# Reordering the end of the mixer stage: convolution taps, the sum of squares and the order of the four output-projection units

## The chip, the cores and the metric

The kernel runs on one core of a Trainium2 chip. The metric is the device time of one execution in microseconds, the median of three runs. The engines of a core run their own instruction lists side by side and meet only at semaphores: PE (TensorE) multiplies matrices, with the weight load (PEld) as a pipelined part of it, DVE (VectorE) and ACT (ScalarE) do elementwise work and empty the PSUM banks, POOL (GpSimd) and SP (SyncE) mostly start transfers. An engine works through its list strictly in order, so an instruction that waits holds up all behind it.

## The reference

A trunk of two layers on 256 tokens of width 1024. Each layer is a mixer and a channel mixer (dense SwiGLU in layer 0, top-2-of-8 experts in layer 1), then an embedding add. This case is about the mixer, which has three head groups that read one projection of the normed input:

```python
def conformer_conv(u, dw_w, dw_b, ln_g, ln_b):          # 256 columns, group "conv"
    val, gate = jnp.split(u, 2, axis=-1)
    h = causal_depthwise_conv(val * jax.nn.sigmoid(gate), dw_w, dw_b)   # 31 taps
    ...  # mean and variance over groups of 64 channels
    hn = ((hg - mu) * lax.rsqrt(var + LN_EPS)).reshape(b, s, c)
    return jax.nn.silu(hn * ln_g + ln_b)

def ssd_mixer(z, xbc, dt_raw, ...):                      # 512 columns, group "SSD"
    y = ssd_chunked(xs, dt, a, bm, cm) + d_skip[:, None] * xs
    yg = y.reshape(b, s, SSD_WIDTH) * jax.nn.silu(z)
    yg = yg.reshape(b, s, SSD_NGROUPS, SSD_WIDTH // SSD_NGROUPS)
    yg = yg * lax.rsqrt(jnp.mean(yg * yg, axis=-1, keepdims=True) + RMS_EPS)
    return yg.reshape(b, s, SSD_WIDTH) * norm_g
```

The third group is latent attention with 4 heads of 64 value columns (256 columns). The three outputs are concatenated to 1024 columns (0 to 255 conv, 256 to 767 SSD, 768 to 1023 attention) and multiplied by `w_out` (1024 x 1024).

## The kernel before, in words

There is one instruction list per engine, written out by hand in the order in which the engine runs it. Weights come through a ring of 7 slots of 128x2048 words. From the output projection on, each unit of weights is parted in two: ACT copies it to `w_hi` (rounded), DVE subtracts to get `w_lo` (`split`, L1221 on ACT and L1640 on DVE), and a product is three matmuls, hi by hi, hi by lo and lo by hi (L509, L510, L511). The slots of `w_hi` and `w_lo` are three each.

The mixer of a layer runs so. PE makes the input projection unit by unit (conv, small columns, four times xbc, two halves of z), and between them the small products of attention and SSD. DVE spreads the 31 taps of the depthwise convolution (`conv_taps`, L1725, two instructions of 128x256 per tap) over the gaps between its other work: taps 0 to 9, 10 to 16, 17 to 19, 20 to 22, 23 to 25 and 26 to 30. The names that matter at the end of the stage:

- `xdd` (DVE L1863) is the input of the chunk state product `st` (PE L701). The decay matrices are multiplied in place (L1869, "mix"), and `yd` (PE L712) reads them. `yo` (PE L719) comes from the state.
- DVE adds yd, yo and the gate into `ytok` (L1874, L1877, L1879, L1882: `ygz_ready`), subtracts the mean of the convolution (L1887), and normalizes attention's output into `ytok` (L1893).
- ACT squares `ytok` for the SSD norm (L1384, Sqrt in L1388: `grm_ready`), and DVE scales `ytok` (L1897, L1901: `ytok_ready`).
- PE transposes `ytok` in three pairs of 128 columns (`y_transposed`, L743): pair j=2 is attention, 0 and 1 are SSD. ACT takes the hi part (`take_yT`, L1397), DVE the lo part (L1646 or L1647).
- The convolution's branch: ACT squares (L1390), PE sums over groups (L752, "var"), ACT takes the root (L1403), DVE inverts and multiplies (L1919, L1920: `chn_ready`), ACT does Silu and the hi copy (L1410, L1413), DVE the lo part (L1646: `yT_ready`).
- The output projection is four units of 24 matmuls, one for each quarter of the 1024 columns, in `OUT_ORDER`: 3 is attention, 1 and 2 SSD, 0 the convolution. All four add into the same four PSUM banks. Unit i waits for its input parts and for `lo_ready` of its weights, which are the splits `f + 10` to `f + 13`.

After the last unit DVE adds the result to `h` (L1930), and the next norm and its transposes (L527) follow.

Of the kernel before, what the change touches and what calls it, by code (L numbers as in the profile page):

```python
# [82 lines left out]
OUT_ORDER = (3, 1, 2, 0)  # L83
# [34 lines left out]
def trunk(nc, params, x, p, positions, w_in, w_uq, w_ukv, w_out, dense_g, dense_u, dense_d, router,  # L118
          moe_g, moe_u, moe_d, ple_g, ple_p, final_g, out):
    with ExitStack() as ctx:  # L120
# [362 lines left out]
        def _(pe):  # L483
# [91 lines left out]
            def mixers(L):  # L575
# [178 lines left out]
                for j in range(2):  # L754
                    pe.wait_ge(ytok_ready, 2 * L + j + 1)
                    y_transposed(j, 1 + j)
                keys = [("o", L, t, half) for t in range(NT) for half in range(2)]
                acc = {}
                for i, pair in enumerate(OUT_ORDER):
                    w = unit()  # L760
                    if i == 0:
                        pe.wait_ge(*banks.taken(("yT", L, 2)))
                    elif i < 3:
                        pe.wait_ge(*banks.taken(("yT", L, i - 1)))
                    else:
                        pe.wait_ge(yT_ready, L + 1)
                    for n, key in enumerate(keys):
# [443 lines left out]
        def _(act):  # L1211
# [18 lines left out]
            def warmed():  # L1230

                act.wait_ge(table_in, warmings[0])
# [46 lines left out]
            def mixers(L):  # L1279
# [29 lines left out]

                act.wait_ge(dtn_ready, L + 1)  # L1310
                A(dte, dtn, ACT.Exp).then_inc(dte_ready, 1)
                A(nega, lp(L, "alog", 0, SH), ACT.Exp).then_inc(nega_ready, 1)
                act.wait_ge(pads_ready, L + 1)
                take_xbc(0)
# [66 lines left out]
                act.wait_ge(ygz_ready, L + 1)  # L1381
                for t in range(NT):
                    for g in range(SG):
                        A(dx[:, t, g * SEQ:g * SEQ + SEQ], ytok[:, t, g * SEQ:g * SEQ + SEQ], ACT.Square,  # L1384
                          accum_out=gss[:, 2 * t + g:2 * t + g + 1]).then_inc(gss_ready, 1)
                act.wait_ge(gss_ready, 4 * (L + 1))
                warmed()
                A(grm, gss, ACT.Sqrt, scale=SG / SSDW, bias=eps_rms).then_inc(grm_ready, 1)  # L1388
# [12 lines left out]
                take_yT(2)  # L1401
                o = banks.filled(act, ("var", L))
                A(csq.rearrange("p m s -> p (m s)"), o, ACT.Sqrt, bias=eps_ln).then_inc(  # L1403
                    banks.is_free(("var", L)), 1)
                for j in range(2):
                    take_yT(j)
# [6 lines left out]
                A(yT_hi[:, 0:2, :], csq, ACT.Copy).then_inc(conv_hi_ready, 1)  # L1413

# [193 lines left out]
        def _(dve):  # L1608
# [101 lines left out]
            def mixers(L):  # L1710
# [64 lines left out]
                conv_taps(10, 17)  # L1775
                xbc_taps(0)
                conv_taps(17, 20)
# [34 lines left out]
                conv_taps(20, 23)  # L1812
                xbc_taps(3)
                split(f + 10)
                conv_taps(23, 26)
# [37 lines left out]
                for t in range(NT):  # L1853
                    for g in range(SG):
                        o = banks.filled(dve, ("seg", L, t, g))
                        for i in range(4):
                            hd = 4 * g + i
                            c = t * SH + hd
                            last = V.tensor_scalar(dec[:, t, hd, :], o[:, i * P:i * P + P], acs[:, c:c + 1], 0.0,
                                                   ALU.subtract, ALU.min)  # L1860
                        last.then_inc(banks.is_free(("seg", L, t, g)), 1)
                dve.wait_ge(ea_ready, L + 1)
# [8 lines left out]
                conv_taps(26, CK)  # L1871
# [24 lines left out]
                dve.wait_ge(grm_ready, L + 1)  # L1896
                step(V.reciprocal(grs, grm))  # L1897
                for g in range(SG):
                    for t in range(NT):
                        v = ytok[:, t, g * SEQ:g * SEQ + SEQ]  # L1900
                        last = V.tensor_scalar(v, v, grs[:, 2 * t + g:2 * t + g + 1], None, ALU.mult)  # L1901
                    last.then_inc(ytok_ready, 1)
# [12 lines left out]
                for j in range(2):  # L1915
                    take_yT(j, 2 + j)
                split(f + 12)
# [4 lines left out]
                rest(yT_lo[:, 0:2, :], csq, yT_hi[:, 0:2, :]).then_inc(yT_ready, 1)  # L1922
                for i in range(13, 16 if L == 0 else 14):
                    split(f + i)
# [376 lines left out]
```

## Time and profile before

| | |
|---|---|
| median of 3 runs | 1562.73 us (1561.97 to 1563.8) |
| profiled execution: its own time | 1562.73 us |
| profiled execution: span of the trace | 1560.9 us |
| busy: PE / DVE / ACT | 1476.2 / 1188.9 / 1013.4 us |
| mean granted TensorE clock | 0.988 |

The span is what the trace shows from the first to the last instruction. The profiled execution took 1.83 us more than its span. Busy time is the time in which an engine had an instruction in work. A timeline row gives the start and the length of one or several like instructions on one engine and, in brackets, how long the engine was idle before it and who released it. The input and mixer stage lies at 0 to 143 us (layer 0) and about 408 us later in layer 1; the dense channel mixer and the embedding lie between, the experts after 578 us.

### The profile page before, as it was taken

The page shows a single profiled execution, that of the slowest core. Times are in us where ns is not written, and L with a number is a line of the kernel's source. Part 1 is how long each engine was busy: PE and PEld are TensorE (multiplying, and loading weights), DVE is VectorE, ACT ScalarE, POOL GpSimd, SP SyncE. Part 2 cuts the span into 40 slices and gives each one's busy share as a digit, 9 for nine tenths or more (in the row PEclk, how much of TensorE's full clock was granted, in tenths as well). Part 3 has the DMA queues.
Part 4 walks back from the last instruction along what each step waited for, and adds up shares of the span by engine and source line. Part 5 has one row for each costly group of instructions (what it writes and reads, how often), then busy time and mean ns, then how long its engine had stood idle before and what let it go on. Part 6 is the DMA issues. An engine that isn't in the chain of part 4 may idle for free.

```text
span 1560.9 us, 18290 instructions
## 1 busy us (share of the span) xinstructions
PE 1476.2 (95%) x6932; PEld 1194.4 (77%) x6932; DVE 1188.9 (76%) x1113; ACT 1013.4 (65%) x947; POOL 9.3 (1%) x21
## 2 busy tenths in 40 slices
PE   6998999999899969999999999999999999999987
PEld 5767888887777758887778887778887778887766
DVE  2796455544457758889998988998979998978994
ACT  3465444434426537768887768887768887768883
POOL 0000000000000000000000000000000000000000
PEclk9999999999999979999999999999999999999999
DMA  8335555555241059999999999999999999999971
GB/s 294 135 109 185 164 188 188 188 189 179 82 137 53 1 198 403 355 356 389 394 395 397 363 348 378 389 394 401 353 354 375 387 401 395 361 354 380 384 289 40
DMA packets 143670, 441.80 MB, mean 283 GB/s; under 512 B 6928, under 2 KB 21296, under 8 KB 143584
## 3 DMA queue, kind: packets, MB, share of 16 engines
q1 hardware_dynamic: 142832, 438.24, 76.1%
q0 software_dynamic: 752, 2.39, 0.4%
q8 instruction: 56, 0.92, 0.2%
q14 instruction: 30, 0.25, 0.0%
HBM read 439.56 MB, written 1.05 MB: 282 GB/s over the span
## 4 chain that ended last, share of the span: by engine, by line
PE 75%; DVE 13%; ACT 7%; issue 5%; DMA 0%; DVEq 0%; ACTq 0%; SPq 0%
PE psum L509 16%; PE psum L511 16%; PE psum L510 16%; DVE w_lo L1640 9%; PE psum L545 5%; ACT w_hi L1221 5%; PE psum L943 4%; PE psum L944 4%; PE psum L559 3%; PE psum L527 2%; PE psum L987 2%; PE psum L902 1%; PE psum L911 1%; PE psum L981 1%; DVE hidden_a L1646 1%
## 5 line engine op out<-in xcount | busy, mean ns | idle before, releaser
L1640 DVE TENSOR_TENSOR w_lo<-ring,w_hi 128x2048 fp32r<-128x2048 f32 x396 | 900.0, 2289 | 241.2 <-ACT w_hi L1221 240.4
L1221 ACT ACTIVATE w_hi<-ring 128x2048 fp32r<-128x2048 f32 x396 | 755.5, 1915 | 283.9 <-PE psum L511 249.5
L511 PE MATMUL psum<-w_hi,hidden_b 128*128 128x512 f32 x560 | 219.1, 391 | 0.0
L943 PE MATMUL psum<-w_hi,xT_parts 128*128 128x512 f32 x448 | 193.3, 431 | 10.9 <-DVE w_lo L1640 10.8
L509 PE MATMUL psum<-w_hi,hidden_b 128*128 128x512 f32 x448 | 178.7, 399 | 7.3 <-DVE w_lo L1640 7.3
L944 PE MATMUL psum<-w_lo,xT_parts 128*128 128x512 f32 x448 | 175.6, 392 | 0.0
L510 PE MATMUL psum<-w_lo,hidden_b 128*128 128x512 f32 x448 | 175.2, 391 | 0.0
L509 PE MATMUL psum<-w_hi,hidden_a 128*128 128x512 f32 x352 | 138.0, 392 | 3.2 <-DVE hidden_a L1646 3.2
L509 PE MATMUL psum<-w_hi,xT_parts 128*128 128x512 f32 x352 | 137.9, 392 | 2.2 <-DVE w_lo L1640 1.8
L511 PE MATMUL psum<-w_hi,xT_parts 128*128 128x512 f32 x352 | 137.1, 389 | 0.0
L510 PE MATMUL psum<-w_lo,xT_parts 128*128 128x512 f32 x352 | 137.0, 389 | 0.0
L510 PE MATMUL psum<-w_lo,hidden_a 128*128 128x512 f32 x352 | 137.0, 389 | 0.0
L511 PEld LDWEIGHTS psum<-w_hi,hidden_b 128*128 128x128 f32 x560 | 105.6, 188 | 22.4
L943 PEld LDWEIGHTS psum<-w_hi,xT_parts 128*128 128x128 f32 x448 | 84.2, 188 | 42.1 <-DVE w_lo L1640 21.2
L509 PEld LDWEIGHTS psum<-w_hi,hidden_b 128*128 128x128 f32 x448 | 84.7, 189 | 26.5 <-DVE w_lo L1640 8.7
L944 PEld LDWEIGHTS psum<-w_lo,xT_parts 128*128 128x128 f32 x448 | 84.3, 188 | 21.1 <-issue 6.2
L510 PEld LDWEIGHTS psum<-w_lo,hidden_b 128*128 128x128 f32 x448 | 84.7, 189 | 16.6
L962 PE MATMUL psum<-w_hi,hidden_a 128*128 128x512 f32 x224 | 92.7, 414 | 4.0 <-DVE w_lo L1640 2.5
L511 PE MATMUL psum<-w_hi,hidden_a 128*128 128x512 f32 x240 | 93.5, 390 | 0.0
L963 PE MATMUL psum<-w_lo,hidden_a 128*128 128x512 f32 x224 | 87.8, 392 | 0.0
L545 PE MATMUL psum<-xT,ring 128*128 128x256 f32 x384 | 84.2, 379 | 0.0
L545 PEld LDWEIGHTS psum<-xT,ring 128*128 128x128 f32 x384 | 72.7, 190 | 11.1 <-issue 1.6
(305 smaller groups left out, 1636.6 us busy)
## 6 DMA issues: line engine op xcount, KB each, us to landing
ring<-in_moe_w_gate SPq DMA_DIRECT2D x112, 1024.0 KB, 7.3
ring<-in_moe_w_up SPq DMA_DIRECT2D x112, 1024.0 KB, 7.5
ring<-in_moe_w_down SPq DMA_DIRECT2D x112, 1024.0 KB, 7.7
ring<-in_w_in SPq DMA_DIRECT2D x16, 1024.0 KB, 5.4
ring<-in_dense_w_gate SPq DMA_DIRECT2D x14, 1024.0 KB, 5.1
ring<-in_dense_w_up SPq DMA_DIRECT2D x14, 1024.0 KB, 5.2
ring<-in_dense_w_down SPq DMA_DIRECT2D x14, 1024.0 KB, 4.8
ring<-in_w_out SPq DMA_DIRECT2D x8, 1024.0 KB, 4.9
```

The source lines that it names most:

```text
L509: mm(o, a[0], b[0], start=first, stop=False)
L510: mm(o, a[0], b[1], start=False, stop=False)
L511: return mm(o, a[1], b[0], start=False, stop=final)
L527: last = mm(o[:, c:c + P], h[:, t, kt * P:kt * P + P], diag[:, t, :], start=True, stop=True)
L545: last = mm(o[:, m * SEQ:m * SEQ + SEQ], w[:, kt, m * P:m * P + P], xT[:, kt, :], start=kt == 0, stop=kt == KT - 1)
L559: last = mm(o[:, 0:n], xT[:, kt, t * P:t * P + P], w[:, q, :], start=kt == 0, stop=kt == KT - 1)
L943: mm(o, xl_hi_lo[kt], w[0][:, q, c], start=kt == 0, stop=False)
L944: last = mm(o, xl_lo_hi[kt], w[1][:, q, c], start=False, stop=kt == KT - 1)
L962: mm(o, elT_hi_lo[kt], w[0][:, q, c], start=kt == 0, stop=False)
L963: last = mm(o, elT_lo_hi[kt], w[1][:, q, c], start=False, stop=kt == FKT - 1)
L1221: A(part(w_hi, g, sizes[g]), raw(g, sizes[g]), ACT.Copy).then_inc(hi_ready, 1)
L1640: V.tensor_tensor(part(w_lo, g, sizes[g]), raw(g, sizes[g]), f32(part(w_hi, g, sizes[g])), ALU.subtract).then_inc(lo_ready, 1)
```

## The change

The change reorders instructions. The count of rows on each engine stays as it was (975 rows on DVE). It has four parts.

1. ACT takes xbc unit 0 (`take_xbc(0)`, L1304 and L1306) ahead of the two Exp for `dt` and the decay rate (L1311, L1312).
2. The convolution's taps are cut otherwise: 10 to 13, 14 to 17, 18 to 20, 21 to 24, and the last six (25 to 30) stand before `xdd` instead of the last five after the mixes.
3. The order of the output projection is attention, convolution, SSD, SSD. PE transposes the two SSD pairs after the first unit.
4. On ACT the squares of `ytok` come after `take_yT(2)`, and `take_yT(0)` and `take_yT(1)` after the convolution's Silu. On DVE `split(f + 11)` and `take_yT(2)` come ahead of the scaling of `ytok`, and the convolution's branch ahead of `split(f + 12)` and the two SSD pairs.

```diff
-OUT_ORDER = (3, 1, 2, 0)
+OUT_ORDER = (3, 0, 1, 2)
@@ PE
-                for j in range(2):
-                    pe.wait_ge(ytok_ready, 2 * L + j + 1)
-                    y_transposed(j, 1 + j)
...
                     if i == 0:
                         pe.wait_ge(*banks.taken(("yT", L, 2)))
-                    elif i < 3:
-                        pe.wait_ge(*banks.taken(("yT", L, i - 1)))
-                    else:
+                    elif i == 1:
+                        for j in range(2):
+                            pe.wait_ge(ytok_ready, 2 * L + j + 1)
+                            y_transposed(j, 1 + j)
                         pe.wait_ge(yT_ready, L + 1)
+                    if i > 1:
+                        pe.wait_ge(*banks.taken(("yT", L, i - 2)))
@@ ACT
+                act.wait_ge(pads_ready, L + 1)
+                take_xbc(0)
                 act.wait_ge(dtn_ready, L + 1)
                 A(dte, dtn, ACT.Exp).then_inc(dte_ready, 1)
                 A(nega, lp(L, "alog", 0, SH), ACT.Exp).then_inc(nega_ready, 1)
-                act.wait_ge(pads_ready, L + 1)
-                take_xbc(0)
...
                 warm_up()
-                act.wait_ge(ygz_ready, L + 1)
...
-                A(grm, gss, ACT.Sqrt, scale=SG / SSDW, bias=eps_rms).then_inc(grm_ready, 1)
                 act.wait_ge(*banks.taken(("mean", L)))
...
                 take_yT(2)
+                act.wait_ge(ygz_ready, L + 1)
...
+                A(grm, gss, ACT.Sqrt, scale=SG / SSDW, bias=eps_rms).then_inc(grm_ready, 1)
                 o = banks.filled(act, ("var", L))
...
-                for j in range(2):
-                    take_yT(j)
                 split(f + 12)
...
                 A(yT_hi[:, 0:2, :], csq, ACT.Copy).then_inc(conv_hi_ready, 1)
+                for j in range(2):
+                    take_yT(j)
@@ DVE
-                conv_taps(10, 17)
+                conv_taps(10, 14)
                 xbc_taps(0)
-                conv_taps(17, 20)
+                conv_taps(14, 18)
...
-                conv_taps(20, 23)
+                conv_taps(18, 21)
                 xbc_taps(3)
                 split(f + 10)
-                conv_taps(23, 26)
+                conv_taps(21, 25)
...
+                conv_taps(25, CK)
                 dve.wait_ge(ea_ready, L + 1)
...
-                conv_taps(26, CK)
```

The end of DVE's list is moved in the same way (part 4), and the rows below show it.

The first place is DVE between the decay matrices and the mixes of a layer (L1859 or L1861 writes the decay matrices, L1863 or L1866 is `xdd`, L1869 or L1872 the four mixes, L1725 or L1727 the taps). Before:

```order
L1859 TENSOR_SCALAR arena_a<-psum,tiny 128x128 [waits full2]
L1859 TENSOR_SCALAR arena_a<-psum,tiny 128x128 x3
L1863 TENSOR_TENSOR xs<-arena_b,tiny 128x512 [waits ea_ready]
L1869 TENSOR_TENSOR arena_a<-arena_a,arena_b 128x512 [waits dec_ready] x4
L1725 SCALAR_TENSOR_TENSOR arena_a<-arena_a,par 128x256 x2
```

After:

```order
L1861 TENSOR_SCALAR arena_a<-psum,tiny 128x128 [waits full2]
L1861 TENSOR_SCALAR arena_a<-psum,tiny 128x128 x3
L1727 SCALAR_TENSOR_TENSOR arena_a<-arena_a,par 128x256 x2
L1727 SCALAR_TENSOR_TENSOR arena_a<-arena_a,par 128x256 [waits dve_step]
L1727 SCALAR_TENSOR_TENSOR arena_a<-arena_a,par 128x256
```

Before, `xdd` and the mixes follow at once and ten tap instructions stand behind them. Now twelve tap instructions stand ahead of `xdd`, of which the first four are shown, and nothing stands between the mixes and L1874.

The second place is the end of DVE's mixer list, from the normalized attention output (L1893 or L1895) on. Before:

```order
L1893 TENSOR_TENSOR xs<-psum,tiny 128x256
L1897 RECIPROCAL tiny<-tiny 128x4 [waits grm_ready]
L1901 TENSOR_SCALAR xs<-xs,tiny 128x256 [waits dve_step]
L1901 TENSOR_SCALAR xs<-xs,tiny 128x256 x3
L1640 TENSOR_TENSOR w_lo<-ring,w_hi 128x2048 [waits hi_ready]
L1646 TENSOR_TENSOR xT_parts<-psum,xT_parts 128x256 [waits full0,y_hi_ready]
```

After:

```order
L1895 TENSOR_TENSOR xs<-psum,tiny 128x256
L1642 TENSOR_TENSOR w_lo<-ring,w_hi 128x2048 [waits hi_ready]
L1648 TENSOR_TENSOR xT_parts<-psum,xT_parts 128x256 [waits full0,y_hi_ready]
L1648 TENSOR_TENSOR xT_parts<-psum,xT_parts 128x256
L1911 RECIPROCAL tiny<-tiny 128x4 [waits grm_ready]
L1915 TENSOR_SCALAR xs<-xs,tiny 128x256 [waits dve_step]
L1915 TENSOR_SCALAR xs<-xs,tiny 128x256 x3
L1918 RECIPROCAL arena_a<-arena_a 128x512 [waits free5]
L1919 TENSOR_TENSOR arena_a<-arena_a 128x512 [waits dve_step]
L1648 TENSOR_TENSOR xT_parts<-arena_a,xT_parts 128x512 [waits conv_hi_ready]
```

The five instructions of the SSD norm moved behind the split and attention's lo part, and the convolution's reciprocal follows them directly. `split(f + 12)` and the SSD pairs come after all of it.

## Rows read from the trace of the kernel before

**Rows 1.** The page's parts 1 and 4: busy time, and the chain by engine.
```profile
PE 1476.2 (95%) x6932; PEld 1194.4 (77%) x6932; DVE 1188.9 (76%) x1113; ACT 1013.4 (65%) x947; POOL 9.3 (1%) x21
PE 75%; DVE 13%; ACT 7%; issue 5%; DMA 0%; DVEq 0%; ACTq 0%; SPq 0%
```

**Rows 2.** Chain in order of time, 105 to 120 us: start, us, what.
```profile
108.63 0.70 DVE xs L1877
...
111.34 0.04 ACT arena_b L1384
```

**Rows 3.** Timeline, 45 to 80 us, ACT and DVE: start, us, engine, line.
```profile
46.47 1.28 ACT L1311 ACT_TABLE_LOAD   x1
...
48.05 0.16 DVE L1773 TENSOR_SCALAR tiny<-tiny 128x16 f32<-128x16 f32 x1
...
52.84 0.60 ACT L1306 ACTIVATE arena_a<-psum 128x512 f32<-128x512 f32 x1
...
62.23 0.18 DVE L1783 TENSOR_TENSOR tiny<-tiny 128x16 f32<-128x16 f32 x1 [1.52 <-ACT tiny L1323]
...
72.52 2.71 DVE L1725 SCALAR_TENSOR_TENSOR arena_a<-arena_a,par 128x256 f32<-128x256 f32 x6
...
79.16 0.88 DVE L1738 SCALAR_TENSOR_TENSOR arena_a<-arena_a,par 128x256 f32<-128x256 f32 x2 [3.93 <-ACT arena_a L1306]
```

**Rows 4.** Timeline, 80 to 111 us: DVE and the PE weight loads.
```profile
83.99 2.71 DVE L1725 SCALAR_TENSOR_TENSOR arena_a<-arena_a,par 128x256 f32<-128x256 f32 x6
...
86.98 0.18 DVE L1818 COPY tiny<-psum 128x24 f32<-128x24 f32 x1 [0.29 <-PE psum L629]
...
99.27 0.68 DVE L1863 TENSOR_TENSOR xs<-arena_b,tiny 128x512 f32<-128x512 f32 x1
...
102.28 4.54 DVE L1725 SCALAR_TENSOR_TENSOR arena_a<-arena_a,par 128x256 f32<-128x256 f32 x10
...
103.02 0.73 PEld L701 LDWEIGHTS psum<-xs,arena_b 128*128 128x128 f32 x4
...
107.45 0.73 PEld L719 LDWEIGHTS psum<-arena_b,arena_a 128*128 128x128 f32 x4
```

**Rows 5.** Timeline, 110 to 130 us: the start of the output projection.
```profile
112.18 0.76 DVE L1893 TENSOR_TENSOR xs<-psum,tiny 128x256 f32<-128x256 f32 x2 [0.16 <-PE psum L734]
...
114.68 2.29 DVE L1640 TENSOR_TENSOR w_lo<-ring,w_hi 128x2048 fp32r<-128x2048 f32 x1
...
114.91 1.04 PE L743 MATMUL psum<-par,xs 128*128 128x128 f32 x8
...
116.88 0.75 DVE L1646 TENSOR_TENSOR xT_parts<-psum,xT_parts 128x256 fp32r<-128x256 f32 x2
...
117.73 0.47 PE L509 MATMUL psum<-w_hi,xT_parts 128*128 128x512 f32 x1 [1.78 <-DVE w_lo L1640]
...
121.31 3.35 DVE L1919 RECIPROCAL arena_a<-arena_a 128x512 f32<-128x512 f32 x1
...
123.27 0.39 PE L509 MATMUL psum<-w_hi,xT_parts 128*128 128x512 f32 x1
...
127.21 0.69 DVE L1646 TENSOR_TENSOR xT_parts<-arena_a,xT_parts 128x512 fp32r<-128x512 f32 x1 [1.82 <-ACT xT_parts L1413]
```

**Rows 6.** Timeline: first projection matmul of layer 1, norm transposes of both layers.
```profile
143.13 6.62 PE L527 MATMUL psum<-xs,h 128*128 128x128 f32 x32 [3.37 <-DVE xs L1632]
...
525.45 0.47 PE L509 MATMUL psum<-w_hi,xT_parts 128*128 128x512 f32 x1 [0.42 <-issue]
...
550.26 3.84 PE L527 MATMUL psum<-xs,h 128*128 128x128 f32 x32 [0.86 <-DVE xs L1632]
```

**Rows 7.** Windows of 1 us: busy time of each engine, granted clock (PEclk), DMA.
```profile
112.00:113.00 1.00, 0.08 (x2) 0.01 (x1) 0.77 (x3) 1.00 (x6) 0.00 (x0) 1.00 0.00 0
148.00:149.00 1.00, 1.00 (x6) 1.00 (x6) 0.69 (x2) 0.35 (x1) 0.00 (x0) 0.50 0.88 244
521.00:522.00 1.00, 0.87 (x5) 0.47 (x4) 0.84 (x4) 1.00 (x4) 0.00 (x0) 0.53 0.00 0
```

More of the change, by code:

```diff
@@ L1380, in mixers @@
                 warm_up()
-                act.wait_ge(ygz_ready, L + 1)
[L1382 to L1387, printed above, removed]
-                A(grm, gss, ACT.Sqrt, scale=SG / SSDW, bias=eps_rms).then_inc(grm_ready, 1)
                 act.wait_ge(*banks.taken(("mean", L)))
@@ L1401, in mixers @@
                 take_yT(2)
+                act.wait_ge(ygz_ready, L + 1)
+                for t in range(NT):
+                    for g in range(SG):
+                        A(dx[:, t, g * SEQ:g * SEQ + SEQ], ytok[:, t, g * SEQ:g * SEQ + SEQ], ACT.Square,
+                          accum_out=gss[:, 2 * t + g:2 * t + g + 1]).then_inc(gss_ready, 1)
+                act.wait_ge(gss_ready, 4 * (L + 1))
+                warmed()
+                A(grm, gss, ACT.Sqrt, scale=SG / SSDW, bias=eps_rms).then_inc(grm_ready, 1)
                 o = banks.filled(act, ("var", L))
@@ L1895, in mixers @@
                 last.then_inc(banks.is_free(("pv", L)), 1)
[L1896 to L1902, printed above, removed]
                 split(f + 11)
@@ L1914, in mixers @@
                 take_yT(2, 1)
-                for j in range(2):
-                    take_yT(j, 2 + j)
-                split(f + 12)
+                dve.wait_ge(grm_ready, L + 1)
+                step(V.reciprocal(grs, grm))
+                for g in range(SG):
+                    for t in range(NT):
+                        v = ytok[:, t, g * SEQ:g * SEQ + SEQ]
+                        last = V.tensor_scalar(v, v, grs[:, 2 * t + g:2 * t + g + 1], None, ALU.mult)
+                    last.then_inc(ytok_ready, 1)
                 dve.wait_ge(*banks.taken(("var", L)))
@@ L1922, in mixers @@
                 rest(yT_lo[:, 0:2, :], csq, yT_hi[:, 0:2, :]).then_inc(yT_ready, 1)
+                split(f + 12)
+                for j in range(2):
+                    take_yT(j, 2 + j)
                 for i in range(13, 16 if L == 0 else 14):
```

## The prediction

> **What bounds the kernel now.** I read the page's busy times first, then the chain, then the timeline around the changed places. PE is busy 95% of the span and is 75% of the chain [rows 1]: the kernel is a row of products, and what a change at another engine is worth shows only where PE has to stand still or is made to run a product later. The chain in order of time shows where that is in the mixer: it runs on PE through the small products and leaves it after yo, whose load is at 107.45 us [rows 4], for DVE's L1877 at 108.6 us [rows 2]. It is back on PE at 117.73 us, where the first projection unit starts after an idle of 1.78 us [rows 5]. From there the four units run without a gap (the 25th matmul, the first of the second unit, starts at 123.27 us, 5.54 us after the first). Before 108 us PE has no wait for DVE at the state product: its weight load stands at 103.02 us, while xdd was written at 99.95 us [rows 4]. So DVE is ahead there by 3.1 us, and behind from 108.6 us on. Layer 1 repeats this 407.72 us later: its first projection matmul is at 525.45 us [rows 6]. Each cost below is taken twice.
>
> All that follows is in the profiled execution's own time, 1562.73 us, of which 1560.9 us are its span and 1.83 us lie outside; that is also the median of the runs.
>
> **Part 1: xbc ahead of the Exp.** DVE's L1773 at 48.05 us waits for the Exp, and all later taps stand behind it. ACT now first waits for the xbc bank, whose evacuation ends at 52.84 + 0.60 = 53.44 us, then loads the table, 1.28 us, and does the Exp (0.22 us, an estimate from the gap of rows 3 between the table load's end at 47.75 us and 48.05 us with the handover). DVE goes on at about 55.0 us, 7.0 late. What covers it: until 79.16 us DVE has two taps fewer, four instructions of 2.71 / 6 = 0.452 us, 1.8 us; and it was idle 1.52 us at 62.23 us. The taps that ended at 75.23 us end at 75.23 + 7.0 - 1.8 - 1.5 = 78.9 us at the latest, and DVE waited for ACT until 79.16 us anyway, 3.93 us [rows 3]. I take 0. If the cover fell short, it would be by tenths, and each tenth would be added to the next part. From below: nothing starts sooner by it, since PE does not wait for xbc here.
>
> **Part 2: the taps.** Four taps instead of three stand before L1818. They would end at 83.99 + 8 x 0.452 = 87.6 us, and L1818 was at 86.98 us: +0.6 us. From there to xdd DVE has no idle worth naming, so xdd is due at 99.9 us. But now twelve tap instructions are ahead of it: 12 x 0.454 = 5.45 us (4.54 us for ten, rows 4). xdd starts at 105.35 and ends at 106.03 us. PE asks for it at 103.02 us, now idles 3.0 us, and all behind it on PE (yd, yo, mean, attention's product) moves by 106.1 - 103.0 = +3.1 us. The mixes, 2.5 us in all, are done at 108.5 us, each one before yd needs it: yd starts 0.8 us after st and takes 3.7 us. The ten tap instructions that stood behind the mixes lay beside yd and cost nothing there (102.28 to 106.8 us, and yo was not before 107.45 us). So the move takes work out of a covered place and puts it in front of PE. The bounds are 0 (had PE been later by 3.1 us) and 5.45 + 0.6 = 6.05 us; I take 3.1 us, since both ends of the wait have a row.
>
> **Part 4 on DVE, up to the first unit.** L1893 ended at 112.94 us and moves with yo to 116.0 us. Behind it the split starts at once; with 116.88 - 114.68 = 2.20 us for it and 0.75 us for attention's lo part the bank is free at 119.0 us and unit 0 starts at 119.1 us [rows 5]. That is +1.35 us against 117.73 us: taking the SSD norm out of the way gives back 1.7 us of the 3.1.
>
> **Part 3, the second unit.** The eight transposes of SSD, 1.04 us [rows 5], ran while PE waited for DVE anyway. Now they stand between unit 0 and unit 1: 119.1 + 5.5 = 124.6 us, then 125.65 us. Unit 1 is now the convolution's and waits for the last step of its branch. That branch is long: from the reciprocal (3.35 us, starts 121.31 us) to the lo part's end (127.90 us) it takes 6.59 us [rows 5]. It can start now when DVE has scaled ytok. PE's four transposes of attention (about 0.6 us, half of the 1.04 and a handover) and ACT's hi part (0.6 us, as L1306 in rows 3) end at about 117.5 us; the four squares, their Sqrt and DVE's scaling take 3.3 us (before, from ACT's first square at 111.34 us [rows 2] to the split behind the scaling at 114.68 us), so about 120.9 us. yT_ready is at 120.9 + 6.6 = 127.5 us, and PE idles about 1.9 us from 125.65 us. Unit 1 starts at 127.55 us instead of 123.27 us: +4.3 us. Had the branch been free, the transposes alone would make it 125.65 us, +2.4 us; with the branch starting later by one split (2.29 us) it would be +6.6 us. I take +4.3 us.
>
> **Units 2 and 3.** DVE does the next split, 2.29 us, and the two SSD pairs, 0.83 us each by the row of attention's 0.75 us, by 131.4 us; PE reaches unit 2 at 133.0 us. They are hidden with 1.6 us to spare. What follows the projection (split, the adds, the norm) is released by PE's units as before. The ring's loads behind `split(f + 12)` on SP's queue start some 8 us later; their weights are used after the norm. So the shift goes on at its full size, into layer 1 and through the experts, where nothing waits for a clock time.
>
> 2 x 4.3 = 8.6 us: 1571.3 us, by the moved instructions alone.
>
> **The clock.** TensorE was granted the lower level (1.2 GHz, 0.50) twice near such idles: at 521 us in layer 1, after a second in which PE did little, and around 142 to 149 us after 3.37 us of idle [rows 6, 7]; yet at 112 us in layer 0, the same place as 521 us, it stayed at 2.4 GHz with PE almost idle for a microsecond. The new idle of 3.0 us at 103 us is nearer to the one of 3.37 us. What it costs: the same 32 transposes took 6.62 us at the lower level and 3.84 us at the full one, so each microsecond at the lower level loses 1 - 3.84 / 6.62 = 0.42 us. The lower level lasted about 5.9 us after work began again at 143.13 us. In the 8.7 us of small products after 106.1 us, all of it ahead of DVE's yo, that is at most 2.5 us and at least 0; I take 5 us, 2.1 us per layer. A fall in the idle of 1.9 us would cost about as much, less likely.
>
> TensorE: Matmul & The Clock Gate of the Trainium skill says in "Part 1: The HAM clock gate" that the throttled state is the default and that activity releases it, so an added idle on PE costs more than its length. The traces agree for two idles and disagree for one. By the rule the sum is 2 x 6.4, without it 2 x 4.3 us.
>
> The sum: 1562.73 + 2 x (4.3 + 2.1) = 1575.5 us.
>
> **Rivals.**
>
> A. The clock stays up at 103 us: 1571.3 us. For it: 112 us, with no fall. Against it: the idle is three times as long.
>
> B. The clock falls at both new idles, in both layers. The second fall costs 2.1 us as well, in units that nothing covers: 1562.73 + 2 x 8.5 = 1579.7 us. For it: in layer 1 a shorter idle was enough. Against it: 24 dense matmuls stand before the 1.9 us.
>
> C. The wait for xdd does not appear, because PE gets to the state product 3.1 us later than I think or DVE has slack that the timeline hides; it decides at 103.02 us. Then unit 0 starts at 116.0 us, 1.7 us earlier than before, its transposes are over at 122.6 us, and the convolution's branch is done at 124.4 us: unit 1 is at 124.5 us, +1.2 us. 1562.73 + 2.4 = 1565.1 us, no change by what can be measured. To be faster the branch must in addition end before the transposes, and then 0.7 us per layer is gained: 1561.3 us. Against it: both sides of the wait have rows, and DVE was without a gap.
>
> D. Part 1 does not stay covered, or an SSD pair is late for unit 2 (DVE has 1.6 us to spare there). If both fail by a microsecond: 1575.5 + 4 = 1579.5 us.
>
> **Chances.** The forecast with a fall at the first idle in one or both layers 0.5; A 0.25; B and D together 0.17; C 0.08. The measurement of this kernel can tell a change of about 0.2%, 3.1 us. C alone lies within it or below; so faster 0.02, same 0.06, slower 0.92. The range of 8 in 10 goes from a little below A, 1569 us, to B, 1580 us.
>
> **What would show it.** DVE should be idle from 48.2 to about 55 us. PE should wait at L701 for about 3 us, released by DVE's xdd. The first projection matmul should start about 1.4 us later than before if the clock held, 3.5 us if not; behind the first 24 there should be eight transposes and an idle of about 2 us released by DVE's lo part of the convolution (little or none of it would say that the branch is quicker than I worked out). The granted clock between 106 and 112 us decides between A and the forecast. I am wrong if xdd stands before 103 us, if unit 1 starts before 125 us, or if the experts' part changes in length.

## The result and the profile after

The changed kernel took 1583.01 us in the median (1580.05 to 1583.84, four runs) and the kernel before 1563.26 us (1561.97 to 1565.76, four runs): a ratio of 1.012, 95% interval 1.0102 to 1.014. A second comparison gave 1581.58 against 1562.79 us, 1.0122 (1.0105 to 1.0139). It is slower, by 19 us; the forecast was 12.8 us and the range ended at 1580 us. The profiled execution was the fastest of the five, 1577.62 us. The page's parts 1 and 4 of the changed kernel:

```profile
span 1575.8 us, 18288 instructions
PE 1483.0 (94%) x6932; PEld 1197.6 (76%) x6932; DVE 1188.2 (75%) x1113; ACT 1013.4 (64%) x947; POOL 9.3 (1%) x21
PE 75%; DVE 13%; ACT 7%; issue 5%; DMA 0%; DVEq 0%; ACTq 0%; SPq 0%
```

The counts are those of before, DVE's and ACT's busy times too [rows 1], but PE was busy 6.8 us longer with the same products: some of them ran slower. The rest of the 14.9 us of span, 8.1 us, is more idle time of PE. The timeline of layer 0, DVE's rows (start, length, and in brackets the idle time ahead and its releaser; L1727 are taps, L1866 `xdd`, L1642 the split, L1648 the lo parts):

```profile
55.23 0.18 DVE L1775 TENSOR_SCALAR tiny<-tiny 128x16 f32<-128x16 f32 x1 [6.87 <-ACT tiny L1314]
...
79.39 0.88 DVE L1740 SCALAR_TENSOR_TENSOR arena_a<-arena_a,par 128x256 f32<-128x256 f32 x2 [1.61 <-ACT arena_a L1306]
...
100.04 5.46 DVE L1727 SCALAR_TENSOR_TENSOR arena_a<-arena_a,par 128x256 f32<-128x256 f32 x12
105.41 0.68 DVE L1866 TENSOR_TENSOR xs<-arena_b,tiny 128x512 f32<-128x512 f32 x1
...
116.00 2.28 DVE L1642 TENSOR_TENSOR w_lo<-ring,w_hi 128x2048 fp32r<-128x2048 f32 x1
118.20 0.75 DVE L1648 TENSOR_TENSOR xT_parts<-psum,xT_parts 128x256 fp32r<-128x256 f32 x2
...
120.70 3.35 DVE L1918 RECIPROCAL arena_a<-arena_a 128x512 f32<-128x512 f32 x1
...
126.59 0.69 DVE L1648 TENSOR_TENSOR xT_parts<-arena_a,xT_parts 128x512 fp32r<-128x512 f32 x1 [1.82 <-ACT xT_parts L1413]
```

The idle of 6.87 us in front of L1775 is the new wait for the Exp. It is gone by L1740 at 79.39 us, where DVE still waits 1.61 us for ACT, as it did before [rows 3]. (This trace is 0.2 us late from its start; each trace has a shift of its own, from 1.5 us earlier to 0.7 us later at L594 in layer 0, which has to be taken off before places are compared.) PE's rows of the same layer:

```profile
106.20 1.10 PE L701 MATMUL psum<-xs,arena_b 128*128 128x256 f32 x4 [2.48 <-issue]
107.14 3.68 PE L712 MATMUL psum<-arena_b,arena_a 128*128 128x64 f32 x32
...
116.14 0.66 PE L743 MATMUL psum<-par,xs 128*128 128x128 f32 x4 [0.92 <-DVE xs L1895]
...
119.04 0.47 PE L509 MATMUL psum<-w_hi,xT_parts 128*128 128x512 f32 x1 [1.39 <-DVE w_lo L1642]
...
124.61 1.04 PE L743 MATMUL psum<-par,xs 128*128 128x128 f32 x8
127.34 0.50 PE L509 MATMUL psum<-w_hi,xT_parts 128*128 128x512 f32 x1 [1.69 <-DVE xT_parts L1648]
```

Layer 0 went as the steps said, to some tenths: the wait at the state product, unit 0 at 119.04 us, the transposes behind it, unit 1 at 127.34 us [rows 4, 5]. The idle is 2.48 us and not 3.0, since PE's products before it run until 103.72 us here. That the 2.48 us at L701 are put down to "issue" must not mislead: no releaser is shown, but DVE's `xdd` ends at 106.09 us and L701 starts at 106.20. The granted clock was 1.00 all the while. Layer 1, the same places:

```profile
516.53 1.10 PE L701 MATMUL psum<-xs,arena_b 128*128 128x256 f32 x4 [2.47 <-issue]
517.47 6.71 PE L712 MATMUL psum<-arena_b,arena_a 128*128 128x64 f32 x32
523.97 2.02 PE L719 MATMUL psum<-arena_b,arena_a 128*128 128x256 f32 x4
...
527.49 3.01 PE L734 MATMUL psum<-arena_b 128*128 128x64 f32 x24
531.41 1.11 PE L743 MATMUL psum<-par,xs 128*128 128x128 f32 x4 [0.92 <-DVE xs L1895]
532.32 1.92 PE L752 MATMUL psum<-arena_a,par 128*128 128x512 f32 x2
```

L712's 32 matmuls took 6.71 us instead of 3.68. The windows (the column after POOL is the granted clock):

```profile
517.00:518.00 1.00, 1.00 (x8) 0.92 (x7) 1.00 (x3) 0.33 (x1) 0.00 (x0) 0.85 0.00 0
518.00:519.00 1.00, 1.00 (x6) 1.00 (x7) 0.83 (x2) 0.98 (x2) 0.00 (x0) 0.50 0.00 0
...
527.00:528.00 1.00, 1.00 (x5) 0.51 (x3) 0.97 (x2) 0.00 (x0) 0.00 (x0) 0.53 0.00 0
528.00:529.00 1.00, 1.00 (x12) 1.00 (x11) 1.00 (x2) 0.00 (x0) 0.00 (x0) 1.00 0.00 0
```

About a microsecond after PE had begun again the clock fell to 0.50 (1.2 GHz), and it stayed there for 10.2 us, from 517.7 to 527.9, though PE had work all the time. From L701 to L743 it is 531.41 - 516.53 = 14.88 us, and in layer 0 116.14 - 106.20 = 9.94: the fall cost 4.94 us.

How the loss adds up along the trace (start of the first matmul of the line named; in the filled version L594 is L601, L527 is L534, L862 is L870 and L902 is L910):

| place | before | after | after, second profile (below) | after with the wait filled (below) |
|---|---|---|---|---|
| layer 0, ahead of the moved instructions' effect (L594) | 59.20 | 59.43 | 58.10 | 58.76 |
| layer 0, behind the projection: the norm's transposes (L527) | 143.13 | 147.33 | 151.41 | 146.65 |
| layer 1, the same (L594) | 466.91 | 469.77 | 475.06 | 470.81 |
| layer 1, behind the projection: gain products (L862) | 547.33 | 559.56 | 564.38 | 555.18 |
| experts' gather (L902) | 567.65 | 580.24 | 585.28 | 576.40 |
| last norm's transposes (L527) | 1525.96 | 1540.85 | 1544.23 | 1534.97 |

From the first row to the second, layer 0's mixer became 3.97 us longer in the first profile (no fall there), 9.38 us in the second and 3.96 us in the filled version; from the third to the fourth, layer 1's became 9.37, 8.90 and 3.95 us longer. So the moved instructions cost 3.96 us in a layer, 7.9 us in all, and a fall the rest. Up to the gain products 12.2 of the 14.9 us have come together. Behind them 2.7 us more came in the first profile: 1.2 us at the experts' start, and 1.5 us at the products of L911, where the granted clock was 0.51 from 1528 to 1530 us and had been 1.00 at the same place of the kernel before. Such a fall at L911 stands in the profile of part 1 alone too (below), and not in the second profile here. Between the experts' start and L911 the expert products took as long as before.

### The profile page after: what moved, and what is told of

Same layout as the page of the kernel before. It is cut to its first block, busy times and chain, and to the rows that moved or that the text cites. A ratio compares the mean times of both kernels' runs of the same rounds, so it can differ in the third digit from the quotient of the medians.

```text
span 1575.8 us, 18288 instructions
## 1 busy us (share of the span) xinstructions
PE 1483.0 (94%) x6932; PEld 1197.6 (76%) x6932; DVE 1188.2 (75%) x1113; ACT 1013.4 (64%) x947; POOL 9.3 (1%) x21
## 4 chain that ended last, share of the span: by engine, by line
PE 75%; DVE 13%; ACT 7%; issue 5%; DMA 0%; DVEq 0%; ACTq 0%; SPq 0%
PE psum L509 16%; PE psum L511 15%; PE psum L510 15%; DVE w_lo L1642 9%; PE psum L545 5%; ACT w_hi L1221 5%; PE psum L943 4%; PE psum L944 4%; PE psum L559 3%; PE psum L987 2%; PE psum L527 2%; PE psum L911 2%; PE psum L902 1%; PE psum L981 1%; DVE hidden_a L1648 1%
## 5 line engine op out<-in xcount | busy, mean ns | idle before, releaser
L1642 DVE TENSOR_TENSOR w_lo<-ring,w_hi 128x2048 fp32r<-128x2048 f32 x396 | 899.7, 2287 | 240.8 <-ACT w_hi L1221 240.0
L943 PEld LDWEIGHTS psum<-w_hi,xT_parts 128*128 128x128 f32 x448 | 84.2, 188 | 42.1 <-DVE w_lo L1642 21.2
L509 PEld LDWEIGHTS psum<-w_hi,xT_parts 128*128 128x128 f32 x352 | 66.2, 188 | 21.8 <-DVE xT_parts L1648 4.1
```

What stands on the lines that cost most here:

```text
L509: mm(o, a[0], b[0], start=first, stop=False)
L943: mm(o, xl_hi_lo[kt], w[0][:, q, c], start=kt == 0, stop=False)
L1642: V.tensor_tensor(part(w_lo, g, sizes[g]), raw(g, sizes[g]), f32(part(w_hi, g, sizes[g])), ALU.subtract).then_inc(lo_ready, 1)
```

## The experiments

All are timed beside the kernel before on the same chip; ratios, not times, are to be compared from one experiment to another. The theory: the moved instructions cost what was worked out, and the clock's fall at PE's new wait costs more than was taken for it. The rivals: the moved instructions cost more (in DVE's later work, or for unit 1), or the four parts hinder one another.

### One part at a time

`taps_only` is the kernel before with part 2 alone:

```diff
-                conv_taps(10, 17) ... conv_taps(17, 20) ... conv_taps(20, 23) ... conv_taps(23, 26)
+                conv_taps(10, 14) ... conv_taps(14, 18) ... conv_taps(18, 21) ... conv_taps(21, 25)
+                conv_taps(25, CK)      # ahead of xdd
-                conv_taps(26, CK)      # behind the mixes
```

> Kernel before with the new cut of the convolution taps alone (10-13, 14-17, 18-20, 21-24, and 25-30 ahead of xdd). Theory T (the wait for xdd costs 3.1 us per layer and then makes the granted clock fall, some 5 us more per layer): 1563 + 2 x 8 = about 1579 us, and in the trace half clock in the small products behind L701 in at least one layer. Rival R1 (the instructions' wait is all that this part costs, the rest of the loss comes from the end of the stage): about 1569 us. Rival R2 (xbc ahead of the Exp is to blame): about 1569 us too.

1573.53 us, ratio 1.0084 (1.0054 to 1.0114). Here it was layer 0 in which the clock fell, PE's rows:

```profile
105.69 1.35 PE L701 MATMUL psum<-xs,arena_b 128*128 128x256 f32 x4 [2.48 <-issue]
106.84 6.93 PE L712 MATMUL psum<-arena_b,arena_a 128*128 128x64 f32 x32
...
120.58 0.65 PE L743 MATMUL psum<-par,xs 128*128 128x128 f32 x4 [0.92 <-DVE xs L1893]
```

14.89 us from L701 to L743 again. In layer 1 of this trace, after the same idle of 2.48 us, L712 took 3.68 us and nothing fell. So the same wait drops the clock in one layer and not in the other, and which one changes. That is one fall where the sum of the expectation had one in each layer (about 1579 us); two of the four executions took 1571.7 us, the others 1575.3 and 1580.1 us.

`tail_only` is the kernel before with parts 3 and 4 (OUT_ORDER and the order of the end of ACT's and DVE's lists):

> Kernel before with the new order of the output projection and of the stage's end on ACT and DVE (parts 3 and 4) alone. Theory T: the branch of the convolution ends late for unit 1, +1.2 us per layer, about 1566 us, first projection matmul at about 116.0 us and unit 1 at about 124.5 us. Rival R1 (the clock falls in the wait between unit 0 and unit 1 and in the emptier end): about 1573 us with half clock in units 1 to 3.

1564.52 us, 1.0016 (1.0006 to 1.0026). Unit 0 was at 115.88 us and unit 1 here:

```profile
124.17 0.50 PE L509 MATMUL psum<-w_hi,xT_parts 128*128 128x512 f32 x1 [1.69 <-DVE xT_parts L1647]
```

That is close to rival C of the prediction in every term (116.0, 124.5 us, +2.4 us), so the convolution's branch and the transposes are priced rightly, to 0.3 us.

`xbc_first_only` is part 1 alone, `take_xbc(0)` ahead of the two Exp:

> Kernel before with ACT taking xbc unit 0 ahead of the two Exp (part 1) alone. Theory T and R1: DVE idles about 7 us at 48 us; with the old cut of the taps the cover is 3.93 + 1.52 + 0.66 + 0.48 = 6.6 us against 7.0, so at most 0.5 us per layer: 1563 to 1565 us. Rival R2: about 1568 us or more.

1562.64 us, 0.9998 (0.9987 to 1.0008): nothing.

The three together are 11.6 + 2.6 us and nothing, 14 us of the 19. The rest is no hindrance of the parts by one another: counted in the traces as in the table above, the mixer is 2.96 and 2.90 us longer with part 2 alone and no fall (`taps_filled`, below) and 1.07 and 1.02 us with parts 3 and 4 alone, together 4.0 us per layer, and all parts at once cost 3.96 us. What differs is the number of falls: one in the two layers of the profile of `taps_only`, three in the four layers of the changed kernel's two profiles. Why there are more with all parts is not shown.

### The wait kept, PE kept busy in it

The changed kernel, with products that nobody reads in PE's wait for `xdd`:

```diff
+            def keep_busy(b, n):
+
+                if banks.count[b]:
+                    pe.wait_ge(banks.free[b], banks.count[b])
+                for _ in range(n):
+                    mm(psum[:, b, :], ones, par[:, 0:512], start=True, stop=True)
...
+                keep_busy(4, n)
                 pe.wait_ge(xdd_ready, L + 1)
```

With n = 6:

> The changed kernel, with six extra matmuls of 128x512 (0.44 us each) on PE into the free bank of st while PE waits for xdd; their results are overwritten. Theory T: the clock stays at the full level in both layers behind L701, and what is left is the instructions' own cost: about 1571 us. Rival R1 (the clock is lost elsewhere, or the fall at xdd is not what costs): it stays at about 1583 us; if the extra matmuls hold PE up, it is more.

1576.3 us, 1.0081 (1.0057 to 1.0105). The clock stayed at 1.00 in both layers, but each call is two instructions of 0.44 us, and the filler was 5.32 us long: it held PE up by itself, and unit 0 was at 121.52 us. The 1571 us that were expected did not come. With n = 3:

> The changed kernel with three products into the state's free bank put in front of PE's wait for xdd, about 2.7 us of work at the higher clock, so that the wait of 2.5 us is filled and not lengthened (six held the first projection unit up to 121.5 us). If the part of the loss above the 8.6 us of moved instructions is the clock's fall after that wait, the granted clock stays 1.00 in both layers from 103 to 115 us, the first projection matmul stands at 119.0 to 119.4 us in layer 0 and at 527 to 528 us in layer 1 (534.3 us in the changed kernel), and the time is 1571 to 1574 us. If the moved instructions alone cost more than worked out (the rival), the clock stays up and the time is still above 1577 us. If small products do not hold the clock, it falls in one layer as before and the time is 1578 to 1583 us.

1569.51 us (1568.7 to 1571.78), 1.0037 (1.0023 to 1.0051). PE's rows of layer 1 (L512 is the filler, L709 the state product, L720 `yd`, L751 the transposes):

```profile
514.94 2.74 PE L512 MATMUL psum<-par 128*128 128x512 f32 x6
517.54 1.13 PE L709 MATMUL psum<-xs,arena_b 128*128 128x256 f32 x4
518.50 3.68 PE L720 MATMUL psum<-arena_b,arena_a 128*128 128x64 f32 x32
...
527.50 0.66 PE L751 MATMUL psum<-par,xs 128*128 128x128 f32 x4 [0.92 <-DVE xs L1903]
```

The state product starts just as late, since `xdd` is no earlier, but it is 9.96 us from L709 to L751, and the time is 12 to 13.5 us less than the changed kernel's, a little under the 1571 to 1574 us expected. Layer 1's first projection matmul, expected at 527 to 528 us, stood at 530.41 us. Part of that is the first profile of the changed kernel, with which it was compared: there the clock had not fallen at layer 0's norm (its 32 transposes took 3.84 us, and 5.47 us here), and the stretch from the second to the third row of the table took 1.7 us less than here. With n = 1:

> The changed kernel with one product (0.9 us) in the wait for xdd instead of three: 1.6 us of idle remain in one piece. If the length of the idle decides whether the clock falls, it falls less often than with 2.5 us: 1571 to 1577 us. If any idle there drops the clock as often, 1580 to 1584 us as in the changed kernel.

1574.68 us (1569.52 to 1580.54), 1.0062 (1.0044 to 1.008). 1.57 us of idle remained. The profiled execution, 1580.54 us, had the fall in both layers; layer 0:

```profile
106.65 1.13 PE L709 MATMUL psum<-xs,arena_b 128*128 128x256 f32 x4 [1.57 <-DVE xs L1874]
107.61 6.17 PE L720 MATMUL psum<-arena_b,arena_a 128*128 128x64 f32 x32
...
121.56 0.66 PE L751 MATMUL psum<-par,xs 128*128 128x128 f32 x4 [0.92 <-DVE xs L1903]
```

14.91 us in each layer (523.23 to 538.14 in layer 1). The fastest execution, at 1569.52 us with a mean clock of 0.992 against 0.983, must have had none; that is read from its mean clock, since it has no profile. By the four times a shorter idle made the fall rarer; by the profile it did not make it cheaper.

The taps' move alone, filled in the same way (n = 3):

> The taps' move alone, with three products (2.7 us) in PE's wait for xdd. The wait itself remains in the time, 3.1 us per layer and 0.6 us of it from the fourth tap: 1562.7 + 6.2 = 1568.9 us. If the clock is what made the taps' move alone cost 11.6 us instead of 6.2, this version takes 1567.5 to 1570.5 us and the granted clock is 1.00 from 103 to 112 us in both layers. If the rest of the 11.6 us is DVE's (a later evacuation, a later norm), it takes 1572 us or more with the clock up.

1568.69 us (1567.95 to 1569.03), 1.0033 (1.002 to 1.0045), where 1568.9 was expected. L751 follows L709 after 9.97 us in both layers. So of part 2's 11.6 us the wait is 5 to 6 (5.4 by these medians, 5.9 by the trace) and the clock the rest. In layer 0 the clock fell later, at the idle of 0.92 us before L751 (0.51 from 117 to 120 us), and it cost nothing: the first unit stands 4.73 us behind L751, and in the kernel before it is 4.74 us behind L743, since PE waits there for DVE anyway.

### The wait taken away

The changed kernel with `conv_taps(25, 28)` ahead of `xdd` and `conv_taps(28, CK)` behind the mixes:

> The changed kernel with six of the twelve tap instructions left ahead of xdd and six behind the mixes. xdd ends 2.7 us earlier, at about 103.3 us, and PE's wait at the state product is 0.3 us or less instead of 3. If the cost is all in that wait and what it does to the clock, then the first unit is at 116.1 us, the second at 124.5 us (the convolution's branch sets it), the clock stays up in both layers, and the time is 1564.5 to 1566.5 us, as the changed tail alone gave. If the clock falls without the wait too, because the other idles of this stretch are enough, the time is 1570 us or more.

1568.03 us (1564.59 to 1569.51), 1.0026 (1.0016 to 1.0035): about 2 us more than worked out. PE had no wait left at L701 (it starts at 102.84 us), but the six taps behind the mixes made the next one longer:

```profile
113.11 1.12 PE L743 MATMUL psum<-par,xs 128*128 128x128 f32 x4 [1.25 <-DVE xs L1896]
114.02 1.92 PE L752 MATMUL psum<-arena_a,par 128*128 128x512 f32 x2
...
124.78 0.50 PE L509 MATMUL psum<-w_hi,xT_parts 128*128 128x512 f32 x1 [2.03 <-DVE xT_parts L1648]
```

1.25 us at L743 instead of 0.92, and in both layers the clock fell at about that place (L752 took 1.92 us and not 1.02). The second half of the expectation ("if the clock falls without the wait too") thus came true in part. Unit 1 is 11.67 us behind L743 in both layers, and 11.20 us in `tail_only`: these falls cost 0.5 us each, through the product of L752, which the convolution's branch waits for. The mixer is 2.1 us longer in each layer than before, 1.0 to 1.1 of it as in `tail_only`; the 0.6 us that are left beside the clock's are DVE's, which gets to L1896 later by the taps.

### The changed kernel a second time

> The changed kernel again, unchanged, for a second profile. In the profiled execution so far (1577.6 us, the fastest of five) the clock fell at the wait for xdd in layer 1 alone and made the stretch from the state product to attention's transposes 14.91 us long instead of 9.97. If the slower executions at 1583 us are those with the fall in both layers, a profile that takes 1580 us or more shows 14.9 us in layer 0 too, and one that takes 1575 to 1578 us shows it in one layer. Rival: the 5 us between them are lost elsewhere (the norm, the experts' start), and a profile above 1580 us still has one such stretch of 9.97 us.

Its profile took 1581.01 us, and the fall is in both layers:

```profile
104.87 1.10 PE L701 MATMUL psum<-xs,arena_b 128*128 128x256 f32 x4 [2.48 <-issue]
105.81 6.86 PE L712 MATMUL psum<-arena_b,arena_a 128*128 128x64 f32 x32
...
119.76 1.11 PE L743 MATMUL psum<-par,xs 128*128 128x128 f32 x4 [0.92 <-DVE xs L1895]
120.66 1.92 PE L752 MATMUL psum<-arena_a,par 128*128 128x512 f32 x2
...
521.84 1.60 PE L701 MATMUL psum<-xs,arena_b 128*128 128x256 f32 x4 [2.48 <-issue]
...
536.72 0.66 PE L743 MATMUL psum<-par,xs 128*128 128x128 f32 x4 [0.92 <-DVE xs L1895]
```

14.89 us in layer 0 and 14.88 in layer 1, as expected of an execution above 1580 us. The windows of layer 0 show 0.50 from 106 to 116 us; the first half:

```profile
106.00:111.00 5.00, 5.00 (x26) 5.00 (x25) 1.87 (x3) 2.08 (x3) 0.00 (x0) 0.50 0.45 169
```

### A version that beats both

Two things in the rows of before pointed to one. PE's first unit waited 1.78 us at 117.73 us [rows 5] for attention's lo part (the row names the split, but the lo part, L1646, ended last, at 117.63 us), which DVE did behind a split of 2.29 us that this unit does not use (it uses `f + 10`). And TensorE ran at the lower level in several stretches behind idles. `lo_first` is the kernel before with one line moved:

```diff
                     last.then_inc(ytok_ready, 1)
-                split(f + 11)
...
                 take_yT(2, 1)
+                split(f + 11)
```

> The kernel before with one line moved: DVE takes attention's lo part before it does the split of the second unit's weights. PE's first unit waited at 117.73 us for whichever of the two came last, and by the order of the units it needs only the lo part. Then attention's lo part ends at 115.4 us, PE has done the eight transposes by 115.9 us, and the first unit starts at 116.0 us instead of 117.7: 1.7 us per layer, 1558.5 us. The second unit then needs the split by 121.5 us (done at 117.7 us) and the first SSD pair (done at 118.5 us). Rival: the split is the first unit's own weights; then nothing starts earlier and the time is the same or 0.7 us per layer longer.

In layer 0 unit 0 started 3.52 us behind DVE's attention rows (L1893 at 112.91, unit 0 at 116.43 us) instead of 5.55 us (112.18 and 117.73): 2.0 us earlier, where 1.7 were expected. The time was 1561.78 us, 0.999 (0.998 to 1.0): 1.3 us less than the kernel before beside it. 1558.5 us were expected, and the interval ends at no change. The rows of layer 1 show why. Of this version:

```profile
518.07 0.99 PE L743 MATMUL psum<-par,xs 128*128 128x128 f32 x4 [0.92 <-DVE xs L1893]
...
522.07 0.48 PE L509 MATMUL psum<-w_hi,xT_parts 128*128 128x512 f32 x1
```

Of the kernel before:

```profile
112.99 0.66 PE L743 MATMUL psum<-par,xs 128*128 128x128 f32 x4 [0.92 <-DVE xs L1893]
...
520.71 0.83 PE L743 MATMUL psum<-par,xs 128*128 128x128 f32 x4 [0.92 <-DVE xs L1893]
```

In both the clock had fallen at the idle of 0.92 us (L752's two products took 2.08 us in each). Before, unit 0 is 4.74 us behind L743 in both layers, with the fall (525.45 us [rows 6]) and without (117.73 us): PE waited for DVE there, so the fall was free. With the lo part early this cover is gone, and unit 0 is 2.71 us behind L743 in layer 0 and 4.00 us in layer 1, where the slow products now decide. Only 0.75 us of the 2.0 were left there.

`before_filled` is the kernel before with fillers in PE's longest idles:

> The kernel before with products of no use put in PE's longest idles ahead of transposes and gathers: three before the norm's transposes in layer 0 (idle 3.37 us), four before the next norm's (4.65 us), seven before the experts' gather (6.99 us) and four behind it (4.81 us). If the clock falls because PE is idle there, it stays at 1.00, the 32 transposes take 3.7 us at 143 us instead of 6.6 and at 422 us instead of 5.4, the gather 3.7 instead of 6.0: about 2.8 + 1.6 + 2.3 us, and some 2 us more in the first expert products, 1554 to 1557 us in all. Rival: the weights' split behind the gather is late whatever the clock, and only 4.4 us or less are gained.

1563.24 us, 0.9992 (0.9982 to 1.0001). Two fillers were wrong. The four meant for the idle of 4.65 us at 422 us stood before another norm's transposes, where PE had no idle, and added 3.60 us; and the seven before the gather met a clock that had already fallen and lasted 8.52 us instead of 6.2 (worked out from the 5.32 us of six calls), longer than the idle. The three before the norm's transposes of layer 0 did what they should:

```profile
139.87 2.74 PE L512 MATMUL psum<-par 128*128 128x512 f32 x6
143.41 3.84 PE L534 MATMUL psum<-xs,h 128*128 128x128 f32 x32 [0.81 <-DVE xs L1645]
```

3.84 us instead of 6.62 [rows 6]. `lo_first_filled` has both, with `keep_busy` of 1 behind attention's product, 3 before the norm in layer 0, 4 at the start of layer 1, 5 before the gather and 3 behind it:

> The kernel before with attention's lo part ahead of the split, and with products of no use in PE's idles, this time no longer than these at the higher clock: one (0.9 us) after attention's product, where PE waits 0.92 us, three (2.7 us) before the norm's transposes in layer 0, four (3.5 us) before the first transposes of layer 1, five before the experts' gather (5.5 us at the lower clock would be 8, so fewer than the seven of the last try) and three behind it. Expected: the clock is kept at 138 to 150 us (2.4 us), at 424 us (1.6 us) and after attention's product (0 to 2 us), and some 2 us come from the experts' start: 1554 to 1558 us, against 1561.8 us with the moved line alone. Rival: the experts' start hangs on DVE and the clock's fall there is not kept off, and 1557.5 us remain; or a filler holds PE up, and the time is 1560 us or more.

1552.74 us (1549.55 to 1556.15), 0.9937 (0.9921 to 0.9952): 10 us faster than the kernel before, and 1554 to 1558 us were expected. Three of the six executions took 1549.6 to 1550.4 us with a mean clock of 0.997 (0.988 before), the others 1555 to 1556.2 us with 0.995. The profiled one is the fastest. In its trace, against the kernel before, the moved line now gives 2.0 us in both layers, the norm of layer 0 2.1, the start of layer 1 1.5 and the experts' start 4.1 us. Its transposes at the start of layer 1 and its gather:

```profile
416.62 3.84 PE L534 MATMUL psum<-xs,h 128*128 128x128 f32 x32 [1.23 <-DVE xs L1647]
...
558.42 3.81 PE L916 MATMUL psum<-arena_b,xs 128*128 128x128 f32 x32 [0.89 <-DVE arena_b L2072]
...
567.04 0.51 PE L516 MATMUL psum<-w_hi,hidden_b 128*128 128x512 f32 x1 [2.23 <-DVE w_lo L1655]
```

The same places of the kernel before:

```profile
422.26 5.36 PE L527 MATMUL psum<-xs,h 128*128 128x128 f32 x32 [4.65 <-DVE xs L1632]
...
567.65 6.00 PE L902 MATMUL psum<-arena_b,xs 128*128 128x128 f32 x32 [6.99 <-DVE arena_b L2057]
578.46 0.80 PE L509 MATMUL psum<-w_hi,hidden_b 128*128 128x512 f32 x1 [4.81 <-DVE w_lo L1640]
```

The time between the products is there as before, with work of no use in it; the products themselves are faster.

## Why the prediction was right in direction and wrong in size

- **Part 1 at nothing: right.** The wait of 6.87 us is in the profile, and the part alone has a ratio of 0.9998.
- **Part 2, the wait of 3 us at the state product: right.** `xdd` at 105.41 us (105.35 was said), and everything behind the wait 2.9 us later in the layer (106.20 us for the product, 103.12 before, less 0.23 of the trace's start), where 3.1 were said. With the clock held part 2 alone costs 5.4 us by the medians and 5.9 by the trace, where 6.2 were said.
- **Part 4 and unit 0: right.** 119.04 us for 119.1; without part 2, 115.88 for 116.0.
- **Part 3 and unit 1: right, a little high.** 127.34 us, of which 0.23 are the trace's start: +3.84 us where 4.3 were said. Behind the projection it is 3.96 us in each layer, 7.9 us in all where 8.6 were said; the filled version's time is +6 us by the ratio (4 to 8).
- **Units 2 and 3 hidden: right. Nothing further in the experts: nearly right.** The expert products between the start and L911 took as long as before. 1.2 us came in at the experts' start in the first profile (1.1 us in the second), and 1.5 us at L911 in the first alone.
- **The clock term: this step failed.** It read "I take 5 us, 2.1 us per layer", with a bound of 2.5 us, which is 5.9 us at the lower level times 0.42 us lost in each. The mechanism was right and both factors were too small: the lower level lasted 10.2 us and cost 4.94 us each time, 0.48 us in each, at six falls in four traces (`after`, `after_again`, `taps_only`, `after_filled_1`). I had carried the 5.9 us and the 0.42 over from one fall at 143 us [rows 6, 7], in other products (transposes, then the dense units), and had called the result a bound. The prediction also put all these products "ahead of DVE's yo", but L725 and L734 stand behind it; their loss is passed on all the same, since attention's transposes wait for L734.
- **How often it falls.** The sum had a fall in each layer at 2.1 us. The first profile has one and the second two: three falls in four passages. With the measured 4.94 us for two falls the recorded sum becomes 1562.73 + 8.6 + 9.9 = 1581.2 us, and the second profile took 1581.01. That so close a hit is in part luck: the instructions cost 7.9 us and not 8.6, and a third fall at L743 (0.5 us), the experts' start (1.1 us) and a trace that is 1.1 us early at its start make up for it.
- **The likelihood.** Rival B (falls at both new idles) did not occur: nothing fell at the idle of 1.7 to 2.0 us before unit 1, in either layer of either profile. So "an added idle on PE costs more than its length" held for one of the two idles that the change added. Rival A's case, no fall in either layer, is what the filled version shows (1569.5 us); in the changed kernel none of the nine executions came near it. One had one fall (1577.6 us), the others took 1579.6 us or more; only one of these was profiled, with two.

Open: by the medians the changed kernel lies 12 to 13.5 us above its filled version, and two falls are 9.9 us. In both profiles of it the clock fell once more at the idle of 0.92 us before L743, in a layer that had just been slow (L752 at 1.92 us), and the filled version's did not; in the convolution's branch this cost 0.5 us. Between the two profiles (the changed kernel's second and the filled version's) the difference from L594 on is just 9.9 us, but the filled version's profile is its slowest execution, 1571.78 us with a mean clock of 0.988. Three of its five executions had 0.992 and took 1568.7 to 1569.5 us: less time at the lower level, at places that no profile shows. The slow stretches at the norms and the gather vary from execution to execution in every version (the 32 transposes of layer 0's norm took from 3.84 to 6.62 us). Nor is it shown what makes the same idle of 2.48 us drop the clock in one layer and not in another.

## What to carry to other kernels

A wait on PE has two prices, its length and what it does to TensorE's clock, and the second can be the larger: here 2.9 us and 4.9 us. One fall elsewhere gives neither the duration nor the loss of the next one (5.9 us at 0.42 there, 10.2 us at 0.48 here), so it is no bound. Ask too whether PE waits for another engine later in the slow stretch: where it does, as at L743 in the kernel before, the fall is free, and taking that wait away brings its price back. Where a wait cannot be removed, products of no use can fill it, as long as they are no longer than it: six calls of 5.32 us and seven of 8.52 us held PE up. Move work of other engines in front of PE's inputs only if PE is late there anyway.

## What the runs showed of the hardware

- After an idle of 2.48 us among small products TensorE went to 1.2 GHz in four of six passages (`after`, `after_again`, `taps_only`), 0.5 to 1.2 us after work had begun again, and stayed there 10.2 us with PE busy all the time; it rose again within the matmuls of L725 or L734. At 143 us, before, the lower level ended 5.9 us after work had begun again [rows 6, 7].
- TensorE: Matmul & The Clock Gate of the Trainium skill says in "HAM oscillation — how this bites in real kernels" that a kernel whose waits throttle PE again and again pays the transition each time, and advises an order that keeps PE warm. The traces agree, with 4.94 us for each fall at the state product, and 5 (part 2 alone) and 12 to 13.5 us (the changed kernel) back when the waits were filled.
- Idles of 0.92 to 1.25 us were sometimes enough: before, layer 1; with the short wait, both layers; in the filled version, neither. Such a fall cost nothing before (unit 0 is 4.74 us behind L743 with it and without) and 0.5 us with the short wait.
- An idle of 1.5 to 2.1 us behind 24 dense matmuls and eight transposes (before unit 1) dropped the clock in none of the profiles.
- The 32 matmuls of 128x64 of L712 took 6.71 to 6.93 us against 3.68, a factor of 1.8 to 1.9, and the two of 128x512 of L752 1.92 us against 1.02.
- A filler has two lengths. Six calls were 5.32 us at the higher level, which makes 6.2 for seven, and seven were 8.52 us where the clock had fallen before they began.
